# VectorE makes the low parts of two neighbouring weight tiles in one instruction

## What is computed

```python
def peer_ffn(x, w_q, sub_keys, expert_u, expert_v):
    q = _rms((xt @ w_q).reshape(T, P_HEADS, P_KEY_DIM))
    s1 = jnp.einsum('thd,hnd->thn', q[..., :half], sub_keys[:, 0])
    s2 = jnp.einsum('thd,hnd->thn', q[..., half:], sub_keys[:, 1])
    v1, i1 = lax.top_k(s1, P_TOPK)                    # 16 of 128 keys, for each token and head
    v2, i2 = lax.top_k(s2, P_TOPK)
    cand = (v1[..., :, None] + v2[..., None, :])      # 256 candidates
    vals, ci = lax.top_k(cand, P_TOPK)
    e = (jnp.take_along_axis(i1, ci // P_TOPK, axis=-1) * N_KEYS
         + jnp.take_along_axis(i2, ci % P_TOPK, axis=-1))   # 16 of 16384 experts
    g = jax.nn.softmax(vals, axis=-1)
    a = jnp.einsum('cd,ckd->ck', xc, expert_u[ec])    # for every chunk of 128 tokens
    w = gc * jax.nn.gelu(a)
    return jnp.einsum('ck,ckd->cd', w, expert_v[ec])
```

## Time and profile before

| | |
|---|---|
| median of three runs | 2191.14 us |
| profiled execution | 2191.93 us |
| its span | 2190.2 us |
| TensorE matmul busy (PE) | 2123.4 us, 97% |
| TensorE weight load (PEld) | 1787.9 us, 82% |
| VectorE (DVE) | 1650.5 us, 75% |
| ScalarE (ACT) | 1044.8 us, 48% |
| GpSimd (POOL) | 635.8 us, 29% |
| low parts (L482) | 398 of 128x1024, 486.0 us busy, 1222 ns each |
| low parts in the part that changes | 254, of jobs 2 to 127 of the up projection and of all 128 of the last stage |

### The profile page before, as it was taken

How to read it: one execution, slowest core, us unless ns; L and a number is a source line. 1 busy time by engine, 2 the same in 40 slices (tenths; PEclk the granted TensorE clock), 3 DMA queues, 4 the chain that set the end, 5 groups by cost and what they waited for, 6 DMA issues and landing times.

```text
span 2190.2 us, 33425 instructions
## 1 busy us (share of the span) xinstructions
PE 2123.4 (97%) x11713; PEld 1787.9 (82%) x11713; DVE 1650.5 (75%) x3228; ACT 1044.8 (48%) x1940; POOL 635.8 (29%) x425
## 2 busy tenths in 40 slices
PE   7999999999999988899999989999998999999999
PEld 6888888888888545687899988999997888888887
DVE  6555555534367687554399999999988999999998
ACT  5333333322243477744455535999844433333332
POOL 0000000000040000020100223777626767767773
PEclk9999999999999999999999999999999999999999
DMA  5322222222325200022355888999989999999996
GB/s 195 97 86 86 86 86 92 82 97 98 98 97 182 78 1 1 1 68 87 125 170 178 281 259 291 377 410 400 395 304 417 419 418 418 418 419 418 419 418 278
DMA packets 137228, 484.57 MB, mean 221 GB/s; under 512 B 15056, under 2 KB 30416, under 8 KB 135184
## 3 DMA queue, kind: packets, MB, share of 16 engines
q1 hardware_dynamic: 75456, 229.93, 29.8%
q0 software_dynamic: 59056, 225.14, 26.0%
q10 hardware_dynamic: 2592, 27.85, 3.1%
HBM read 435.42 MB, written 46.92 MB: 220 GB/s over the span
## 4 chain that ended last, share of the span: by engine, by line
PE 79%; DVE 17%; ACT 2%; issue 1%; DMA 0%; ACTq 0%; DVEq 0%
PE bank L1257 24%; PE bank L495 15%; PE bank L496 15%; PE bank L497 15%; DVE rows L2327 5%; DVE wlo L482 3%; DVE hot L2485 2%; PE bank L510 2%; DVE hot L2483 2%; PE bank L610 1%; PE bank L570 1%; PE bank L813 1%; PE bank L831 1%; ACT pair_prob L1479 1%; PE bank L1211 1%
## 5 line engine op out<-in xcount | busy, mean ns | idle before, releaser
L495 PE MATMUL bank<-act_hi,whi 128*128 128x320 f32 (+1 forms) x1840 | 646.6, 351 | 23.2 <-DVE wlo L482 19.8
L496 PE MATMUL bank<-act_lo,whi 128*128 128x320 f32 (+1 forms) x1840 | 635.3, 345 | 0.0
L497 PE MATMUL bank<-act_hi,wlo 128*128 128x320 f32 (+1 forms) x1840 | 635.0, 345 | 0.0
L482 DVE TENSOR_TENSOR wlo<-raw,whi 128x1024 fp32r<-128x1024 f32 x398 | 486.0, 1222 | 140.4 <-ACT whi L478 138.2
L478 ACT ACTIVATE whi<-raw 128x1024 fp32r<-128x1024 f32 x398 | 417.9, 1056 | 341.4 <-PE bank L1257 203.9
L495 PEld LDWEIGHTS bank<-act_hi,whi 128*128 128x128 f32 x1840 | 346.2, 188 | 65.6 <-DVE wlo L482 23.4
L497 PEld LDWEIGHTS bank<-act_hi,wlo 128*128 128x128 f32 x1840 | 346.0, 188 | 32.8
L496 PEld LDWEIGHTS bank<-act_lo,whi 128*128 128x128 f32 x1840 | 346.4, 188 | 31.6 <-issue 0.7
L762 POOL DMA_INDIRECT rows<-peer_u,idxU x128 | 194.4, 1519 | 330.7 <-DVE udot L2327 158.8
L1257 PE MATMUL bank<-whi,h_hi 128*128 128x512 f32 x768 | 237.9, 390 | 7.2 <-issue 7.2
L1257 PE MATMUL bank<-wlo,h_hi 128*128 128x512 f32 x768 | 237.8, 390 | 0.0
(11 more groups left out here) (403 smaller groups left out, 2929.2 us busy)
## 6 DMA issues: line engine op xcount, KB each, us to landing
raw<-tiles SPq DMA_DIRECT2D x398, 512.0 KB, 4.9
gates_dram<-stage ACTq DMA_DIRECT2D x12, 2048.0 KB, 11.3
wg<-gates_dram POOLq DMA_DIRECT2D x16, 1536.0 KB, 17.1
acts_dram<-gelu SPq DMA_DIRECT2D x120, 160.0 KB, 5.0
hf<-acts_dram POOLq DMA_DIRECT2D x30, 640.0 KB, 13.5
bias<-alibi POOLq DMA_DIRECT2D x16, 256.0 KB, 3.0
w1s<-cmp_w POOLq DMA_DIRECT2D x1, 4096.0 KB, 12.9
res<-x_t ACTq DMA_DIRECT2D x4, 512.0 KB, 6.7
```

The lines of the kernel that those rows point to most:

```text
L482: dve.tensor_tensor(wlo[:, j.slot, :], raw[:, j.slot, :], whi[:, j.slot, :].bitcast(F32), ALU.subtract).then_inc(lo_made, 1)
L495: pe.matmul(to, wh, x, start=(kc == 0), stop=False)
L496: pe.matmul(to, wh, xl, start=False, stop=False)
L497: last = pe.matmul(to, wl, x, start=False, stop=(kc == KC - 1))
```

## The change

A new function makes two low parts with one instruction over two neighbouring slots, 128x2048 numbers. It waits for both high parts and then counts both low parts as made. It is called at every even job, where the low part of that job stood, and the low part at the odd job goes away: in the first jobs and the token tiles (through `u_job`), in the turns of the gates, in the last 8 jobs of the up projection, and in the last stage. 127 instructions of 128x2048 take the place of 254 of 128x1024. The stages before the up projection keep `make_lo`. Nothing changes in what the other engines issue.

```diff
+        def make_two_lo(dve, j):
+            two = slice(j.slot, j.slot + 2)
+            dve.wait_ge(hi_made, j.n + 2)
+            dve.tensor_tensor(wlo[:, two, :], raw[:, two, :], whi[:, two, :].bitcast(F32),
+                              ALU.subtract).then_inc(lo_made, 2)
...
             def u_job(n):
-                make_lo(dve, Job(J_U + n).ahead())
+                if n % 2 == 0:
+                    make_two_lo(dve, Job(J_U + n).ahead())
...
-                make_lo(dve, Job(J_U + U_GATES + q).ahead())
+                if q % 2 == 0:
+                    make_two_lo(dve, Job(J_U + U_GATES + q).ahead())
                 if q < EXTRA_Q:
                     for _ in range(DOTS_GATES * q // EXTRA_Q, DOTS_GATES * (q + 1) // EXTRA_Q):
                         use_row()
             for n in range(KEPT):
-                make_lo(dve, Job(J_U + U_REST + n).ahead())
+                if n % 2 == 0:
+                    make_two_lo(dve, Job(J_U + U_REST + n).ahead())
...
             for jj in range(P):
-                if jj + AHEAD < P:
-                    make_lo(dve, Job(J_V + jj).ahead())
+                if jj % 2 == 0 and jj + AHEAD < P:
+                    make_two_lo(dve, Job(J_V + jj).ahead())
```

## The result

The changed kernel takes 2235.25 us, the median of six runs from 2231.12 to 2239.8 us; the kernel before takes 2191.59 us over the same number of runs. The ratio is 1.0198, its 95% interval 1.0184 to 1.0213. The runs after scatter more (8.7 us, 2.4 before), and why isn't settled. The sign was forecast, the size not: the forecast was 2218.4 us, with a range to 2230. The profiled execution after has a span of 2234.2 us, 44.0 us more than before.

A forecast was written before the change was run, and what follows sets the result against it. VectorE was taken to set the up projection's pace, TensorE the last stage's. Token tiles 12.0, gates 11.0, entry 3.3 and last stage 1.0 made 27.3 us on 2191.9, or 2218.4 from the runs' median; range 2202 to 2230, chance 0.78.

The forecast's parts named there:

- What the pair costs and saves: VectorE: a pair takes 2.23 us to the next start against 2.28, saving 0.05 us, bounds 0 and 0.08.
- Token tiles: First jobs and token tiles: VectorE's waits for the second high part make 12.0 us of lateness, bounds 6 and 13.
- jobs 46 and 48: Token tile 2: VectorE's wait for the second high part adds 2.6 us at the first, 2.1 at the second.
- the half instruction: Token tile 0: where TensorE waits for an even low part, that part ends a whole half later, 1.1 us.
- Gates: 48 gate turns, 20 pairs with dots: shared waits of 0.6 us a pair, 11.0 us after savings, bounds 6 to 22.
- Into the last stage: Pair of jobs 122 and 123 starts later, VectorE's dots end later: 3.3 us passed on, bounds 0 and 5.9.
- The last stage: TensorE never waits; VectorE enters 4 us late, pairs save 2.9 by job 116: 1.0 us lost, bounds 0 to 4.
- The last of the prediction's signs: If the stretch to 1584 us is right and TensorE waits in the last stage, the last term is mis-sized.
- The 1.5 us at job 116: Last stage: this low part ended 1.5 us ahead of TensorE; pairs would need 2.2, so 0.7 us is lost.
- Rival 4: Last stage can't hold a pair, even low parts stall TensorE, gates share nothing: 2231 to 2240 us, chance 0.07.
- Rivals 1 to 3: 1: high parts punctual, about 2189 (0.07); 2: TensorE slack, within 4 us of 2191 (0.04); 3: gates share waits, 2196 (0.04).
- The rule of the Trainium skill: Up projection: grouping can improve throughput of a saturated engine; by that alone 2.8 us saved, time 2188.

The follow-up runs named there:

- The two-singles kernels: Changed kernel with two 128x1024 instructions at the pair's place instead of one 128x2048: behind one wait for both high parts 2221.85 us, each behind its own 2204.23 us.
- early high parts: ScalarE makes the high part of job n+4 right behind the gelu of job n; in the kernel with pairs in the gates alone (2207.19 us), 2190.13 us.

## Why the prediction was right and wrong

**What the pair costs and saves.** 2.20 us from start to start against 2.23 forecast. Right, with the saving at its upper bound; it matters little.

**Token tiles, 14.4 us for 12.0,** outside the bound of 13. The running sum came near: 1.2 us after jobs 2 and 3 (1.1), 4.8 at job 22 (4.6), 7.3 at job 32 (5.8), 8.3 at job 48 (8.4), 11.3 at job 50 (10.5). That is partly luck. The forecast had waits of VectorE at jobs 46 and 48, where the pairs wait for nothing; the pair of jobs 44 and 45 waits 4.88 us instead. It had no term for the clock, which makes half of the 14.4. And it named VectorE's standing as the cause nearly throughout and the half instruction once, with 1.1 us. The two-singles kernels give VectorE's standing 3.8 us, the even part's wait 4.6, the half instruction 6.0. The sum came out by adding the pair's whole duration to the arrival of the second high part, which holds all three.

**Gates, 13.6 us for 11.0.** The mechanism is shown: with ScalarE's high part moved, or the pair one place later, it's gone. The size came near. The waits aren't shared as I had it, though: one pair waits 1.0 to 2.3 us and the next hardly at all, 12.7 us in 9 times between 1400 and 1607 us.

**Into the last stage, 6.1 us for 3.3,** just outside the bound of 5.9 (4.4 in the kernel with pairs in the up projection alone). By exclusion it belongs to the pairs of the last 8 jobs: pairs in the gates alone, entering 15 us late, lose 0.3 us there.

**The last stage, 9.7 us for 1.0 with a bound of 4: the step that failed.** I read TensorE's 521.8 of 522 us in the earlier trace rows and concluded that the stage is TensorE's, with VectorE's lead as slack. The last of the prediction's signs points at it: TensorE now waits there. The last columns of that row, a DMA share of 1.00 and 405 GB/s, I didn't read. The 1.5 us at job 116 I took for a thin place; it was the end of a stock that had drained from 10. And I let the 0.05 us that each pair was to save make up for the late start; the saving never became lead, which stayed at 4.1 to 4.3 us where no row was late and drained where rows were. Rival 4 forecast 2231 to 2240, where the result lies, and its mechanism, that low parts with little lead stall TensorE, is what happened in the last stage, at four of them. Its number was partly luck: it also asked for gates that share nothing, and they cost 13.6 us, not over 20. What I held against it, that the waits for row landings take up lateness, was the wrong way round: with a full DMA they are the lateness.

**Rivals 1 to 3** fell: high parts were not there in time, and TensorE had no slack for it. The rule of the Trainium skill (Perfetto Trace Analysis, section Optimizing Scalar/DVE Operations) that grouping can help a saturated engine fell here too: VectorE was busy 98% of the up projection, grouping saved 0.08 us a time, and the joined waits cost many times that. Where the second producer is early, the loss at least goes away, with early high parts or the pair one place later; a gain from grouping isn't shown.

## What to carry to other kernels

An instruction that does the work of two waits for the later of two producers and is ready for the earlier of two consumers only when the whole is done; price both, and ask first whether the later producer can be moved ahead or the joined instruction put at the later place. Where a ring of four buffers is used in twos, the lead that it can hold falls (here from 10 to 6 us at the start and 4 further on), so read how the lead runs through the stage and what drains it, not only its value at one place. And read every column of the stage's row: here TensorE was at 100% and the DMA full too, and the 33 us that VectorE had free in the last stage were no slack, only its lead was. Last, look at the granted clock when TensorE begins to stand: here the stops in the token tiles cost about as much again in matmuls that ran at half clock behind them.

## What the runs showed of the hardware

The DMA's share alone doesn't say that it holds up the stage. With 14 MB less to move, the first three quarters of the stage read, in the kernel with single low parts:

```profile
1662.00:1792.00 130.00, 130.00 (x562) 107.34 (x563) 122.58 (x156) 49.69 (x80) 87.96 (x63) 0.98 1.01 403
1792.00:1922.00 130.00, 130.00 (x575) 107.68 (x574) 124.21 (x142) 49.97 (x80) 87.92 (x63) 1.00 1.00 393
1922.00:2052.00 130.00, 130.00 (x576) 107.64 (x575) 125.18 (x126) 50.56 (x81) 94.70 (x64) 1.00 1.00 392
```

The share is still 1.00, at 392 to 403 instead of 418 GB/s, but no row lands late and the lead doesn't drain. What tells them apart is VectorE's wait for landings, and the lead.
